# Three transformer blocks on one core: a reordered launch, and the rounding of weights in two halves

## The chip, the core and the metric

One Trainium2 chip, one of its cores. The time is the device time of one execution in microseconds (us), the median of the runs. TensorE (PE) multiplies, VectorE (DVE) and ScalarE (ACT) work element by element, GpSimd (POOL) rounds the weights, and SyncE (SP) only issues transfers. An engine waits for another on a semaphore.

## The reference, cut to what matters

Three residual blocks run over a sequence of 512 tokens with 1024 features, in fp32. The start of the first block is what the launch computes:

```python
def rmsnorm(x, g):
    y = xf * lax.rsqrt(jnp.mean(xf * xf, axis=-1, keepdims=True) + EPS)
    return (y * g).astype(x.dtype)

def short_conv_mixer(xn, w_in, conv_w, w_out):
    b, c, h = jnp.split(xn @ w_in, 3, axis=-1)
    return (b * causal_dwconv(c * h, conv_w)) @ w_out
# block 1: x += short_conv_mixer(rmsnorm(x)); x += conv_ffn(rmsnorm(x))
# block 2: forgetting attention (16 heads, own k/v norm), conv_ffn
# block 3: gated linear attention and sliding-window attention (8 heads, sinks), merged by
#          two sigmoid gates, w_out; then a gated feed-forward layer
```

The matrices hold about 186 MB in all, and each is read once.

## The kernel before, in words

Activations are kept with features on the 128 partitions: XT[:, m, :] is feature tile m (128 features) by 512 tokens, eight tiles in all. An fp32 product is made of three fast products: every operand is split into a high part rounded to fp32r and a low part, the rest. XH and XL are the split of x times the norm's gain; the factor of each token, rsqrt(mean(x*x)), is applied later, to the result of a product, as the row W[0].

A weight unit is [128, 8 x 128] (some have 6 x 128): 354 of them. For each, SP loads it into RAW[slot] (L439) when the slot's last unit is split, POOL makes the high part (L468, one operand), waits for its own semaphore `high_done`, makes the low part (L470, two operands) and then raises `split_done`; POOL waits for `unit_done` before it writes a ring slot again. The ring has four slots, in some phases three. In loops POOL also issues one tiny operation (L467). PE's `unit` (L485 to 487) takes 8 x 3 matmuls of 512 columns.

The launch is written out by hand, in this order of each engine's queue:

- SP: four loads of x (XIN, 512 KB each), then the units' weights.
- ACT: the load of the constants (CST), 18 small loads of parameters (L1523) into the rows PROW and one more (L1524); then `residual("_x")`: for each tile a square (L1149) and a high part XH (L1151); then `norm("_x")`.
- PE: three transposes of PROW after all the parameters have come; then for each tile m four transposes (L1098) of XIN into bank m % 2, each pair of banks freed by DVE's copy; then the first products of the loop `mix`, whose three units per step go to banks 0, 1 and 2. After the first unit, `row_sums` (L498) adds up the squares over the partitions.
- DVE: constants, parameters (L2153 to 2159), then for each tile: the copy of PS into XT (L2165), the sum of squares (L1587, L1590), the low part XL (L1593); then the norm (L1567, Newton's step L1557 and L1558, with ACT's Ln, Exp, Square at L1131 to 1133 between).

PE may begin the first unit when `resid` counts all eight copies.

The prediction also speaks of one place of the sliding-window part: for head group g and block q, `swa_scores`, DVE's maximum (L2007), small sums (L2010, L2016, L2017), four scalings of the probabilities SPROB (L2019), then PE's transposes of these (L974, `swa_turn_probs`). Around it DVE also does norms of q and k (L1966, L1969).

## Time and profile before

| | |
|---|---|
| median of 3 runs | 2167.97 us (2167.3 to 2170.32) |
| the profiled execution | 2167.74 us, of which the span of the trace is 2165.7 us |
| PE busy | 2119.7 us (98%) |
| POOL busy | 1285.0 us (59%), 907 instructions |
| DVE busy | 1164.8 us (54%), 1520 instructions |
| ACT busy | 432.6 us (20%) |
| DMA | 193.44 MB, mean 89 GB/s |

The profile's page gives busy times by engine; busy time of PE is modelled, so idle time and the distance between starts say more than it. Views of the trace: the timeline lists instructions in order of time, the waits who stood idle for whom, the groups by line the mean duration of an operation, the stretches the busy time and the granted TensorE clock in a window.

### The profile page before, as it was taken

To read this page: it belongs to the slowest core of one execution; us is meant where nothing else is said; L and a number is where in the kernel's file an instruction comes from. 1 tells how busy PE (TensorE), PEld (TensorE's weight loads), DVE (VectorE), ACT (ScalarE), POOL (GpSimd) and SP (SyncE) were. 2 spreads that over 40 slices of the span, in tenths; PEclk is the share of its full clock that TensorE was granted. 3 is DMA by queue.
4 is the path that set the end of the run, shared out by engine and by line. 5 is a ranking of instruction groups with operands and counts; after the bars stand their busy time and mean duration, and the time that the engine had idled before them with its cause. 6 is when DMAs were issued, how large, how long until landed. Compare 5 with 4: busy or idle time off the path is not lost.

```text
span 2165.7 us, 29143 instructions
## 1 busy us (share of the span) xinstructions
PE 2119.7 (98%) x10839; PEld 1768.7 (82%) x10847; DVE 1164.8 (54%) x1520; ACT 432.6 (20%) x879; POOL 1285.0 (59%) x907
## 2 busy tenths in 40 slices
PE   5999999999999999999999999999999999999999
PEld 4888888888788887888888888889877888888887
DVE  5557777731546666687762167345754455444200
ACT  2002111100243334211110053222223112111000
POOL 3777766656653344676666755435534666666564
PEclk9999999999999999999999999999999999999999
DMA  4333333323332221333323432223222333333232
GB/s 125 97 107 107 90 96 96 94 81 94 110 109 79 79 79 49 109 100 95 96 73 102 115 85 70 68 59 88 68 64 64 88 100 95 97 97 97 73 97 83
DMA packets 368005, 193.44 MB, mean 89 GB/s; under 512 B 6592, under 2 KB 364320, under 8 KB 367920
## 3 DMA queue, kind: packets, MB, share of 16 engines
q1 hardware_dynamic: 364272, 186.67, 30.0%
q10 hardware_dynamic: 3648, 5.59, 0.8%
q8 instruction: 58, 0.95, 0.2%
q14 instruction: 27, 0.22, 0.0%
HBM read 190.11 MB, written 2.13 MB: 89 GB/s over the span
## 4 chain that ended last, share of the span: by engine, by line
PE 86%; DVE 8%; issue 3%; ACT 2%; ACTq 0%; DMA 0%; DVEq 0%
PE PS L485 20%; PE PS L486 20%; PE PS L487 20%; DVE W L1590 2%; PE PS L762 2%; PE PS L778 2%; PE PS L763 2%; PE PS L764 2%; PE PS L779 2%; PE PS L780 2%; PE PS L664 2%; PE PS L665 2%; PE PS L666 2%; PE PS L578 1%; PE PS L847 1%
## 5 line engine op out<-in xcount | busy, mean ns | idle before, releaser
L470 POOL TENSOR_TENSOR RING<-RAW,RING 128x1024 fp32r<-128x1024 f32 (+1 forms) x354 | 870.2, 2458 | 29.5
L468 POOL TENSOR_SCALAR RING<-RAW 128x1024 fp32r<-128x1024 f32 (+1 forms) x354 | 379.0, 1071 | 518.0 <-PE PS L487 147.8
L485 PE MATMUL PS<-XH,RING 128*128 128x512 f32 x1344 | 526.5, 392 | 5.6 <-DVE XT L2165 2.6
L486 PE MATMUL PS<-XL,RING 128*128 128x512 f32 x1344 | 523.5, 390 | 0.0
L487 PE MATMUL PS<-XH,RING 128*128 128x512 f32 x1344 | 523.5, 389 | 0.0
L485 PEld LDWEIGHTS PS<-XH,RING 128*128 128x128 f32 x1344 | 252.7, 188 | 61.7 <-DVE XT L2165 3.0
L486 PEld LDWEIGHTS PS<-XL,RING 128*128 128x128 f32 x1344 | 252.8, 188 | 53.1 <-issue 1.2
L487 PEld LDWEIGHTS PS<-XH,RING 128*128 128x128 f32 x1344 | 252.7, 188 | 52.7
L467 POOL TENSOR_TENSOR COL<-COL 128x1 f32<-128x1 f32 x195 | 44.9, 230 | 314.7 <-PE PS L487 314.7
L485 PE MATMUL PS<-HH,RING 128*128 128x512 f32 x528 | 205.6, 389 | 0.0
L487 PE MATMUL PS<-HH,RING 128*128 128x512 f32 x528 | 205.4, 389 | 0.0
L486 PE MATMUL PS<-HL,RING 128*128 128x512 f32 x528 | 205.4, 389 | 0.0
L1601 DVE TENSOR_TENSOR XT<-PS,XT 128x512 f32<-128x512 f32 (+1 forms) x48 | 33.2, 692 | 312.8 <-PE PS L487 312.7
L1631 DVE TENSOR_TENSOR HL<-W,HH 128x512 f32 (+1 forms) x66 | 117.2, 1775 | 58.7 <-ACT HH L1166 58.7
L778 PE MATMUL PS<-RING,XH 128*128 128x256 f32 x448 | 129.7, 290 | 0.9 <-DVE SGA L1892 0.9
L779 PE MATMUL PS<-RING,XH 128*128 128x256 f32 x448 | 126.7, 283 | 0.0
L780 PE MATMUL PS<-RING,XL 128*128 128x256 f32 x448 | 126.6, 283 | 0.0
L1163 ACT ACTIVATE W<-W 128x512 f32<-128x512 f32 x66 | 41.8, 633 | 415.2 <-DVE W L1608 341.5
L487 PEld LDWEIGHTS PS<-HH,RING 128*128 128x128 f32 x528 | 99.1, 188 | 20.6
L486 PEld LDWEIGHTS PS<-HL,RING 128*128 128x128 f32 x528 | 99.1, 188 | 20.6
L485 PEld LDWEIGHTS PS<-HH,RING 128*128 128x128 f32 x528 | 99.1, 188 | 20.5
L1607 DVE SCALAR_TENSOR_TENSOR W<-W,FC,W 128x512 f32<-128x512 f32 x44 | 104.0, 2364 | 6.0 <-DVE W L1606 1.7
(299 smaller groups left out, 3385.1 us busy)
## 6 DMA issues: line engine op xcount, KB each, us to landing
RAW<-in_ffn_w_up SPq DMA_DIRECT2D x88, 512.0 KB, 3.7
RAW<-in_w_in SPq DMA_DIRECT2D x53, 512.0 KB, 3.7
RAW<-in_w_ffn_in SPq DMA_DIRECT2D x44, 512.0 KB, 3.8
RAW<-in_ffn_w_down SPq DMA_DIRECT2D x32, 512.0 KB, 4.0
RAW<-in_a_w_in SPq DMA_DIRECT2D x24, 512.0 KB, 3.7
RAW<-in_w_kvf SPq DMA_DIRECT2D x17, 512.0 KB, 4.0
RAW<-in_b_w_qg SPq DMA_DIRECT2D x16, 512.0 KB, 3.7
RAW<-in_w_ffn_out SPq DMA_DIRECT2D x16, 512.0 KB, 3.8
```

The source lines that it names most:

```text
L467: pool.tensor_tensor(TICK, ONEC, ONEC, ALU.mult)
L468: pool.tensor_scalar(WH[s][:, 0:nk, :], RAW[s][:, 0:nk, :], 1.0, 1.0, ALU.mult, ALU.mult).then_inc(high_done, 1)
L470: pool.tensor_tensor(WL[s][:, 0:nk, :], RAW[s][:, 0:nk, :], WH[s][:, 0:nk, :].bitcast(F32), ALU.subtract).then_inc(split_done, 1)
L485: pe.matmul(o, WH[s][:, k, :], xh[:, k0 + k, :], start=first and k == 0, stop=False)
L486: pe.matmul(o, WH[s][:, k, :], xl[:, k0 + k, :], start=False, stop=False)
L487: mm = pe.matmul(o, WL[s][:, k, :], xh[:, k0 + k, :], start=False, stop=last and k == nk - 1)
L664: pe.matmul(o, xh[:, k, c], RING[:, s:s + 2, 0, k, :], start=k == 0, stop=False)
L778: pe.matmul(o, XH[:, k, c], RING[:, s:s + 2, 0, k, :], start=k == 0, stop=False)
L779: pe.matmul(o, XH[:, k, c], RING[:, s:s + 2, 1, k, :], start=False, stop=False)
L780: mm = pe.matmul(o, XL[:, k, c], RING[:, s:s + 2, 0, k, :], start=False, stop=k == KT - 1)
L1607: link(dve.scalar_tensor_tensor(o, x[:, 1:S + 1], w[1], o, ALU.mult, ALU.add))
L1631: dve.tensor_tensor(tile(HL, m), g, tile(HH, m).bitcast(F32), ALU.subtract).then_inc(sem("ffn_low"), 1)
```

## The change

Two edits. The first reorders the launch. SP issues the first weight unit, then the four x loads, then the other units; each x load has a semaphore of its own. The 16 rows of `attn_norm` get a buffer GROW and a load right after the constants. PE transposes them into bank 7, then transposes x block by block of 128 tokens as each arrives, into all eight banks; nothing frees a bank in between. XH and XL are made straight from PSUM: ACT squares the first three token blocks (128 x 1024, summed along the row by the instruction), then makes the eight XH, then squares the fourth block. DVE makes XL from PSUM and later copies PSUM into XT ("keep"), six tiles; ACT copies two. The token factor is computed on [128, 4] values and brought to a row by a product of ones with a diagonal matrix, after the second unit. The other parameters are transposed after the first unit, in bank 3. Tests on semaphores are renumbered (`tables`, `params`, `prm_ready`), with no other effect.

The second edit is in POOL's loop: k tiles 0 to 3 and 4 to the end are rounded one after the other, high, low, high, low, each with its wait; `split_done` comes after the second low part.

The core of the diff (renumbered waits and allocations left out):

```diff
@@ sync
+            def load_x():
+                for t in range(TB):
+                    sp.dma_start(XIN[:, t, :], ...).then_inc(sem(f"x_loaded{t}"), 16)
             for p in ph.values():
 ...
+                        if p is ph["mix"] and isinstance(i, int) and i == j == 0:
+                            load_x()
@@ gpsimd
-                        pool.tensor_scalar(WH[s][:, 0:nk, :], RAW[s][:, 0:nk, :], 1.0, 1.0, ALU.mult, ALU.mult).then_inc(high_done, 1)
-                        pool.wait_ge(high_done, p.unit(i, j) + 1)
-                        pool.tensor_tensor(WL[s][:, 0:nk, :], RAW[s][:, 0:nk, :], WH[s][:, 0:nk, :].bitcast(F32),
-                                           ALU.subtract).then_inc(split_done, 1)
+                        for h, (k0_, k1) in enumerate(((0, 4), (4, nk))):
+                            hi = pool.tensor_scalar(WH[s][:, k0_:k1, :], RAW[s][:, k0_:k1, :], 1.0, 1.0, ALU.mult, ALU.mult)
+                            hi.then_inc(high_done, 1)
+                            pool.wait_ge(high_done, p.unit(i, j) * 2 + (h + 1))
+                            lo = pool.tensor_tensor(WL[s][:, k0_:k1, :], RAW[s][:, k0_:k1, :],
+                                                    WH[s][:, k0_:k1, :].bitcast(F32), ALU.subtract)
+                            if h:
+                                lo.then_inc(split_done, 1)
@@ tensor
-            pe.wait_ge(sem("params"), 16 * N_PARAM_DMAS)
 ...
-            for m in range(KT):
-                if m >= 2:
-                    pe.wait_ge(sem("resid"), tiles("_x") + m - 1)
-                for t in range(TB):
-                    tr = pe.transpose(PS[:, m % 2, t * P:(t + 1) * P], XIN[:, t, m * P:(m + 1) * P], ...)
-                tr.then_inc(sem("xt"), 1)
+            pe.wait_ge(sem("consts"), 32)
+            pe.transpose(PS[:, 7, 0:2 * KT], GROW[:, :], ...).then_inc(sem("prm_t"), 1)
+            for t in range(TB):
+                pe.wait_ge(sem(f"x_loaded{t}"), 16)
+                for m in range(KT):
+                    if t == 0 and m == KT - 1:
+                        pe.wait_ge(sem("prm_ready"), 2)
+                    tr = pe.transpose(PS[:, m, t * P:(t + 1) * P], XIN[:, t, m * P:(m + 1) * P], ...)
+                    if t == TB - 1:
+                        tr.then_inc(sem("xt"), 1)
-            pe.wait_ge(sem("resid"), tiles("_x") + KT)
+            def param_rows():
+                pe.wait_ge(sem("params"), 16 * (N_PARAM_DMAS + 1))
+                pe.wait_ge(sem("zeroed"), 1)
+                pe.wait_ge(sem("kept_v"), 2)
+                for l in range(3):
+                    tr = pe.transpose(PS[:, 3, P * l:P * l + P], PROW[:, l, :], CST[:, C_ID:C_ID + P])
+                tr.then_inc(sem("prm_t"), 1)
             def mix(i):
+                first = isinstance(i, int) and i == 0
                 for j in range(3):
+                    if first:
+                        pe.wait_ge(*((sem("kept_v"), 1), (sem("kept_s"), 1), (sem("kept_s"), 2))[j])
 ...
+                    unit(p, i, j, j, XH, XL, ready=(sem("xld"), 1, 0) if first and j == 0 else None)
+                    if first and j == 0:
+                        param_rows()
+                    if first and j == 1:
+                        pe.wait_ge(sem("diag"), TB)
+                        pe.wait_ge(sem("kept_v"), 6)
+                        pe.matmul(PS[:, 7, :], ONE[:, :], DIAG[:, :], start=True, stop=True).then_inc(sem("nsum"), 1)
@@ scalar
             act.dma_start(CST[:, :], T["consts"][:, 0:C_GF]).then_inc(sem("consts"), 16)
+            act.dma_start(GROW[:, :], T["attn_norm"].rearrange("l (k p) -> (l k) p", p=P)).then_inc(sem("consts"), 16)
 ...
-            residual("_x", 1, KT, [(XH, XL, R_ATTN)])
-            norm("_x")
+            def square_x(t):
+                act.wait_ge(sem(f"x_loaded{t}"), 16)
+                act.activation(SQX[:, t, :], XIN[:, t, :], ACT.Square, accum_out=XSS[:, t:t + 1]).then_inc(sem("x_sq"), 1)
+            for t in range(3):
+                square_x(t)
+            act.wait_ge(sem("prm_ready"), 2)
+            for m in range(KT):
+                act.wait_ge(sem("xt"), m + 1)
+                act.activation(XH[:, m, :], PS[:, m, :], ACT.Copy, scale=PRM[:, R_ATTN + m:R_ATTN + m + 1]).then_inc(sem("xhd"), 1)
+            square_x(3)
+            rsqrt(XSS, XR, XRR, sem("nv"), 1, sem("nrr"))
+            for m in (1, 2):
+                act.wait_ge(sem("xld"), m + 1)
+                act.copy(XT[:, m, :], PS[:, m, :]).then_inc(sem("kept_s"), 1)
@@ vector
-            residual("_x", 1, KT, [(XH, XL, R_ATTN)], take_x, ahead=True)
-            norm("_x")
+            dve.tensor_copy(PRM[:, R_ATTN:R_ATTN + 2 * KT], PS[:, 7, 0:2 * KT]).then_inc(sem("prm_ready"), 1)
+            dve.wait_ge(sem("prm_ready"), 2)
+            def keep(m):
+                dve.tensor_copy(XT[:, m, :], PS[:, m, :]).then_inc(sem("kept_v"), 1)
+            for m in range(KT):
+                dve.wait_ge(sem("xhd"), m + 1)
+                dve.scalar_tensor_tensor(XL[:, m, :], PS[:, m, :], PRM[:, R_ATTN + m:R_ATTN + m + 1],
+                                         XH[:, m, :].bitcast(F32), ALU.mult, ALU.subtract).then_inc(sem("xld"), 1)
+                if m == 0:
+                    keep(0)
+            dve.wait_ge(sem("x_sq"), TB)
+            dve.tensor_scalar(XSS, XSS, 1.0 / D, EPS, ALU.mult, ALU.add).then_inc(sem("nv"), 1)
+            keep(3)
+            keep(4)
+            keep(5)
+            newton(XSS, XR, XRR, sem("nrr"), 1, XR)
+            for t in range(TB):
+                dve.tensor_scalar(DIAG[:, t * P:(t + 1) * P], IDF[:, :], XR[:, t:t + 1], None, ALU.mult).then_inc(sem("diag"), 1)
+            keep(6)
+            keep(7)
+            dve.wait_ge(sem("prm_t"), 2)
 ...
+            dve.wait_ge(sem("nsum"), 1)
+            link(dve.tensor_copy(W[0][:, 0:S], PS[:, 7, :]))
```

## Rows read from the trace of the kernel before

**Rows 1.** The page, busy time by engine.

```profile
PE 2119.7 (98%) x10839; PEld 1768.7 (82%) x10847; DVE 1164.8 (54%) x1520; ACT 432.6 (20%) x879; POOL 1285.0 (59%) x907
```

**Rows 2.** Waits of PE: line, waited for, us in total, times, longest.

```profile
PE PS L1088 <- DMA PROW<-in_ffn_conv: 12.9, 1, 12.9
PE PS L1098 <- DVE XT L2165: 7.0, 5, 3.0
PE PS L974 <- DVE SPROB L2019: 5.7, 1, 5.7
PE PS L664 <- DVE KN L1685: 2.2, 1, 2.2
```

**Rows 3.** Timeline of the launch: start, duration, engine, line, operation, idle before.

```profile
8.44 0.36 ACTq L1524 DMA_DIRECT2D TINY<-in_swa_sinks  x1
11.27 1.05 POOL L468 TENSOR_SCALAR RING<-RAW 128x1024 fp32r<-128x1024 f32 x1 [10.82 <-DMA RAW<-in_a_w_in]
14.91 1.28 ACT L1149 ACT_TABLE_LOAD   x1 [14.91 <-DVE PRM L2159]
16.21 0.63 ACT L1149 ACTIVATE W<-XT 128x512 f32<-128x512 f32 x1
16.74 0.71 ACT L1151 ACTIVATE XH<-XT,PRM 128x512 fp32r<-128x512 f32 x1
24.48 0.74 DVE L1593 SCALAR_TENSOR_TENSOR XL<-XT,PRM,XH 128x512 fp32r<-128x512 f32 x1
31.46 0.80 PE L485 MATMUL PS<-XH,RING 128*128 128x512 f32 x1 [2.61 <-DVE XT L2165]
```

**Rows 4.** The same timeline: POOL's tiny operation, released by a unit's last matmul.

```profile
39.00 0.20 POOL L467 TENSOR_TENSOR COL<-COL 128x1 f32<-128x1 f32 x1 [16.86 <-PE PS L487]
45.24 0.19 POOL L467 TENSOR_TENSOR COL<-COL 128x1 f32<-128x1 f32 x1 [2.56 <-PE PS L487]
50.68 0.19 POOL L467 TENSOR_TENSOR COL<-COL 128x1 f32<-128x1 f32 x1 [1.75 <-PE PS L487]
```

**Rows 5.** ACT's groups by line and shape: busy us, mean ns, idle before.

```profile
L1220 ACT ACTIVATION_READ_ACCUMULATOR PROB<-PROB,COL 128x1 f32 x64 | 12.0, 187 | 0.0
L1131 ACT ACTIVATE TINY<-TINY 128x8 f32<-128x8 f32 (+1 forms) x26 | 5.3, 206 | 58.5 <-DVE TINY L1676 32.8 <-DVE TINY L1969 25.7
```

**Rows 6.** POOL's groups by line and shape, columns as in rows 5.

```profile
L470 POOL TENSOR_TENSOR RING<-RAW,RING 128x1024 fp32r<-128x1024 f32 x330 | 825.4, 2501 | 27.5
L468 POOL TENSOR_SCALAR RING<-RAW 128x1024 fp32r<-128x1024 f32 x330 | 358.8, 1087 | 511.6 <-PE PS L487 141.3 <-PE PS L780 118.2 <-PE PS L666 112.8
L470 POOL TENSOR_TENSOR RING<-RAW,RING 128x768 fp32r<-128x768 f32 x24 | 44.8, 1866 | 2.0
L468 POOL TENSOR_SCALAR RING<-RAW 128x768 fp32r<-128x768 f32 x24 | 20.2, 842 | 6.4 <-PE PS L487 6.4
```

**Rows 7.** Timelines of DVE, POOL and PE in the sliding-window part.

```profile
1558.50 1.60 DVE L1969 SCALAR_TENSOR_TENSOR TINY<-TINY 128x4 f32<-128x4 f32 x1
1565.26 1.85 DVE L2016 TENSOR_TENSOR COL<-COL 128x4 f32<-128x4 f32 x1
1567.35 6.94 DVE L2019 TENSOR_SCALAR SPROB<-SPROB,COL 128x384 f32<-128x384 f32 x4
1643.27 1.41 DVE L2019 TENSOR_SCALAR SPROB<-SPROB,COL 128x384 f32<-128x384 f32 x4
1567.05 1.05 POOL L468 TENSOR_SCALAR RING<-RAW 128x1024 fp32r<-128x1024 f32 x1
1571.73 2.34 POOL L470 TENSOR_TENSOR RING<-RAW,RING 128x1024 fp32r<-128x1024 f32 x1
1574.34 2.82 PE L974 MATMUL PS<-IDF,SPROB 128*128 128x128 f32 x12 [5.68 <-DVE SPROB L2019]
1648.99 1.47 PE L974 MATMUL PS<-IDF,SPROB 128*128 128x128 f32 x12
```

**Rows 8.** Stretch 1573 to 1578: busy us by engine, granted clock, DMA share, GB/s.

```profile
1573.00:1578.00 5.00, 3.66 (x15) 3.46 (x16) 3.17 (x4) 1.17 (x2) 1.07 (x1) 0.52 0.57 149
```

More of the change, by code:

```diff
@@ L218, in build @@
         CST = at("CST", [P, C_GF], F32, BIG + 18 * KB)
+        SQX = at("SQX", [P, TB, D], F32, BIG + 64 * KB)
+        GROW = at("GROW", [2 * KT, P], F32, W_at[9])
+        DIAG = at("DIAG", [P, S], F32, W_at[3])
+        XSS, XR, XRR = [TINY[:, c:c + TB] for c in (48, 52, 56)]
         BUH = at("BUH", [P, KT, S], F32R, BIG + 32 * KB)
@@ L550, in body @@
                             unit(pu, i, 2 * q + k, 2 * q + k, XH, XL,
-                                 ready=(sem("xld"), 1, tiles(n)) if isinstance(i, int) and i == 0 and q == k == 0 else None)
+                                 ready=(sem("xld"), 1, scaled(n)) if isinstance(i, int) and i == 0 and q == k == 0 else None)
                             if isinstance(i, int) and i == 0 and q == k == 0:
@@ L692, in attention @@
                 pe.wait_ge(sem("resid"), tiles(1) + KT)
-                unit(p, 0, 0, 0, XH, XL, ready=(sem("xld"), 1, tiles(1)))
+                unit(p, 0, 0, 0, XH, XL, ready=(sem("xld"), 1, scaled(1)))
                 row_sums(1)
@@ L886, in gla @@
                 pe.wait_ge(sem("resid"), tiles(3) + KT)
-                unit(ph["lr"], 0, 0, 4, XH, XL, ready=(sem("xld"), 1, tiles(3)))
+                unit(ph["lr"], 0, 0, 4, XH, XL, ready=(sem("xld"), 1, scaled(3)))
                 row_sums(3)
@@ L1106, in mix @@
                         pe.wait_ge(sem(f"mix_{'chb'[j]}"), i * 1)
-                    unit(p, i, j, j, XH, XL, ready=(sem("xld"), 1, tiles("_x")) if isinstance(i, int) and i == 0 and j == 0 else None)
-                    if isinstance(i, int) and i == 0 and j == 0:
-                        row_sums("_x")
+                    unit(p, i, j, j, XH, XL, ready=(sem("xld"), 1, 0) if first and j == 0 else None)
[5 more added lines that the diff above has]
+                        pe.matmul(PS[:, 7, :], ONE[:, :], DIAG[:, :], start=True, stop=True).then_inc(sem("nsum"), 1)
@@ L1135, in norm @@
             def norm(n):
-                rsqrt(W[4][:, 0:S], W[5][:, 0:S], W[6][:, 0:S], sem("nv"), ORDER[n] + 1, sem("nrr"))
+                rsqrt(W[4][:, 0:S], W[5][:, 0:S], W[6][:, 0:S], sem("nv"), ORDER[n] + 2, sem("nrr"))
             def residual(n, iters, tpi, gains):
@@ L2207, in PARAM_DMAS @@
     d = []
-    for row, a in ((R_ATTN, T["attn_norm"]), (R_FFN, T["ffn_norm"]), (R_ACONV, T["a_conv"][0])):
+    for row, a in ((R_FFN, T["ffn_norm"]), (R_ACONV, T["a_conv"][0])):
         n = a.shape[0] * a.shape[1] // P
@@ L2224, in PARAM_DMAS @@
     return d
-N_PARAM_DMAS = 3 + 8 + 4 + 1 + 2
+N_PARAM_DMAS = 2 + 8 + 4 + 1 + 2
 def constants():
```

57 lines of the change are left out of this document (25 added, 32 removed).

## The prediction, made before the changed kernel was run

> **What bounds the kernel now.** I read the page first: PE is busy for 98% of the span [rows 1], so 46 us of the 2165.7 are all that can be had without fewer matmuls. The waits of PE come next: the two longest lie in the launch, for the last small parameter load and for DVE's copies out of PSUM, and behind them stand one wait of 5.7 us for SPROB and one of 2.2 for KN [rows 2]. Then the timeline of the launch: the first product starts at 31.46 [rows 3], and POOL's tiny operation, which starts right after a unit's last matmul, marks the ends of the first three units at 39.00, 45.24 and 50.68 [rows 4]. So a unit costs 50.68 - 45.24 = 5.44 us when nothing stops it, and the row sum between the first two costs 6.24 - 5.44 = 0.8. Nowhere in PE's waits does POOL stand as the cause: beside the four of [rows 2] there are 14 groups, of 0.2 to 2.6 us, and they name DVE or only issue. Last, the timeline of the one long wait later on [rows 7].
>
> The time outside the span is 2167.74 - 2165.7 = 2.0 us and stays. The profiled execution lies 0.2 us under the median.
>
> **Part 1, the launch.** What it removes: PE's wait for 18 parameter loads ahead of x, the eight rounds through two banks, the sum of squares on DVE (eight operations, some of them long), and the copy into XT ahead of XL. What takes its place is a chain through ACT, which I add up in time.
>
> - x. W0, x and the constants are the same bytes that before had landed when POOL began at 11.27 [rows 3]; only their order is turned round. So the last x block lands at about 11.2. POOL gets W0 ahead of the first x block and has split it long before 15; nobody waits for that.
> - ACT issues its loads until 8.44 + 0.36 = 8.80 [rows 3]; the load of GROW takes the place of another. Its table load is 1.28: until 10.1. In before it came right after a wait; here it may be ahead of it, which changes nothing since block 0 is there by then.
> - Three squares of 128x1024. No such row exists. A square of 512 takes 0.63 [rows 3], twice that is 1.26 from above; the start of the next one 0.53 later (16.21 to 16.74, rows 3) gives 1.06 from below; with 0.19 for the read of the sum [rows 5], if it isn't overlapped, 1.06 to 1.45. I take 1.3: until 14.0. The last x block is transposed by then: 8 transposes behind 11.2.
> - Eight XH at 0.53 apart to 0.71 each [rows 3], taken as 0.6: until 18.8. The first one is there at 14.7, DVE's first XL (0.74, rows 3) at 15.5, and PE can begin the first unit at 15.5 instead of 31.46.
> - Fourth square 1.3 (20.1), table for Ln 1.28 (21.4), Ln 0.21, table for Exp 1.28, Exp and Square 0.21 each (23.3) [rows 3, 5], then the copy of XT tile 1 out of bank 1, 0.6 to 0.7 by the ACT rows of that size: 24.0. The second unit waits for this copy. Queued behind ACT's squares are XH, and so DVE and PE; behind the rsqrt are the two copies.
>
> PE's own path to that point: the first unit from 15.5. It took 39.00 - 31.46 = 7.5 us before [rows 3, 4], against 5.44 when nothing stops it; DVE's XL (eight of 0.74 and one keep of about 0.7) set no less than 6.6 + 0.7. Until 22.8 to 23.0, and three transposes behind, at most 0.9: 23.9. The two paths meet at 24.0, so unit 2 starts at 24.1. It ends at 29.6, the sum by ones and DIAG 0.8, the third unit 5.44: 35.9, against 50.68. **That is 14.8 us.** What could be late inside: DIAG. DVE has newton's results at 23.6, then four operations in SBUF while POOL splits the fourth unit (from 23.0, about 3.7 us), then two keeps: done at 28 if each loses 0.8, at 30 if each loses 1.25. So 0 to 0.5 us on the path; I take 0. The first products are read by DVE after the third unit has started, as before; nothing that follows in the loop depends on when it began. Bounds of part 1: squares and XH at their ends give +-1.6; DIAG 0.5; PE as the later path 1. So 12 to 16.5 us.
>
> **Part 2, POOL's halves.** Price on POOL: from 1024 to 768 columns the low part falls from 2501 to 1866 ns and the high part from 1087 to 842 [rows 6]: 2.48 and 0.96 ns per column, the fixed part 0 and 0.1. Two halves are thus 2 x (1.24 + 0.60) = 3.7 against 3.59, and one more wait for its own semaphore, 0.1 at most. POOL's unit becomes 3.7 to 4.0 us, 354 of them 40 to 140 us more work. Who covers it: PE needs 5.44 per unit [rows 4]; POOL is idle for 880 us of the span [rows 1]. So nothing on the path, while the cover holds. If it didn't, each unit would cost the difference.
>
> Gain on DVE: at 1567.35 the four scalings of SPROB last 6.94 us; the same four last 1.41 at 1643.27 [rows 7]. In between POOL rounds two units without a pause, from 1567.05 to 1571.73 + 2.34 = 1574.07, and DVE's last one ends at 1574.29. Four POOL operations, four DVE operations: each of DVE's gets in only where one of POOL's ends. With pieces of half the length the four get in within 3.6 to 3.9 us, 3.2 less. Ahead of them in the same chain stand operations on four elements that last 1.60 and 1.85 [rows 7]; they too lose about half, 1.6 together. DVE is ready 4.8 us earlier, and PE's wait of 5.68 shrinks to about 0.9. The wait had a second price: in the window behind it the granted clock was 0.52 [rows 8], the same 12 transposes lasted 2.82 instead of 1.47 [rows 7], and some matmuls behind them ran slower too: 1.3 to 1.8 us, which a wait of 0.9 wouldn't bring. Against it: the first weight unit of that part is split only when the doubles before it are done, so POOL's longer unit can hold PE by 0 to 0.5 once; but then PE comes later to the wait for SPROB, so it is in the sum already. **About 6 us**, between 2 and 7.5. The other waits for DVE, KN [rows 2] and twelve smaller ones, some 11 us together, are behind chains of which only a part is held by POOL: 0.8 us, between -1 and 3.
>
> What the trace shows of the price of DVE's getting in: POOL's two units took 7.02 us in that stretch, no more than 2 x 3.59 by their means. DVE's four operations cost it nothing.
>
> The Trainium skill's page "SBUF — State Buffer" (section "SBUF: two separate sides") says that DVE and GpSimd share a port pair that is locked for a whole instruction, by whichever starts first, and that the other is fully blocked. For DVE the rows agree. By the same rule POOL would be blocked at each of its doubled boundaries as well, which speaks against the change: with it the sum would be that of the third rival, below. The 7.02 us do not show it.
>
> **Sum.** 2167.74 - 14.8 - 6 - 0.8 = 2146.1; against the median, 2146.4.
>
> **Rivals.**
>
> *The halves bring nothing.* DVE's chain is then as long as before, because POOL's pieces are back to back and DVE is held by the next one as well, or what DVE wins POOL loses. For it: the chain has ACT operations between DVE's. Against it: four for four in the rows. Time: 2167.97 - 14.8 = 2153, from 2151 to 2156.
>
> *The launch brings much less.* The ACT chain is the new bound, and it is all in one queue. If the parameters' wait comes back (GROW behind the constants and x), or ACT's squares wait for late blocks because W0 is ahead of x, everything moves by that; Against it: W0 is 0.5 of the 2.9 MB that have landed by 11.27, so each block comes at most 2 us later than before, and the third still ahead of its square at 12.7. A further table load in the chain would be 1.28. Launch 9 to 12, halves as forecast: 2149 to 2153.
>
> *Slower: POOL becomes the bound in the feed-forward phases.* There DVE has, per two units, five operations that work in SBUF alone, each of the size of XL's 0.74 [rows 3] or less. If each of them blocks POOL at a boundary, POOL's two units take 2 x 3.85 + 5 x 0.7 = 11.2 us, and PE's 10.88. It decides from 5.44 us per unit on. The loss is 0.16 us and, with loop overhead, perhaps 0.3 for each of about 200 feed-forward units: 32 to 60 us, less the launch: 2167.97 - 14.8 + 32 = 2185 and up. Against it: the 7.02 us, and that POOL idles 512 us ahead of its high parts alone, and more ahead of its tiny operation, released by PE [rows 4, 6].
>
> This is what the Trainium skill's rule on the port pair, named above, would give if it held for POOL as it does for DVE.
>
> *More.* Several of the ten small waits go and the chain on ACT is at its lower ends: 2138 to 2141.
>
> **How the numbers follow.** Forecast 0.60 (2141 to 2150), halves without effect 0.17, launch with less 0.12, more 0.07, slower 0.04. The range that leaves out about 2 in 10 and takes in the bounds is 2139 to 2156. A difference of 0.2%, 4.3 us, is about what a measurement of this kernel tells from none. Faster by more: 0.94; within: 0.02; slower: 0.04.
>
> **What would show it.** In the profile after: the first product near 15.5 and POOL's tiny operations ending the first units near 23, 29.7 and 36; ACT's squares at 1.1 to 1.4 us; the second unit released by ACT's copy or just behind the three transposes. POOL's pieces near 0.6 and 1.24 us, with more busy time but no waits of PE for POOL; the four scalings of SPROB below 4.2 us, and PE's wait there near 1. Wrong would be: a first unit after 18; a second unit held past 25; PE waits on POOL; SPROB's wait over 3.

## The result, and the profile after

The changed kernel takes 2137.76 us (median of 4 runs, 2137.62 to 2138.7) against 2167.98 for the kernel before in the same session; the ratio is 0.9858, with a 95% interval of 0.9845 to 0.9872. The profiled span fell from 2165.7 to 2135.9 us, by 29.8. The forecast was 2146.4 with a range from 2139 to 2156, so the result lies 1.2 us below the range: the sign and the two main mechanisms were right, one term was much too small.

The page after, busy time by engine, to be read against [rows 1]:

```profile
PE 2113.4 (99%) x10840; PEld 1766.9 (83%) x10848; DVE 968.7 (45%) x1516; ACT 431.5 (20%) x881; POOL 1503.7 (70%) x1615
```

DVE does nearly the same instructions and is busy for 196 us less; POOL is busy for 219 us more. Some of the longest waits of PE after (line, waited for, us in total, times, longest), against [rows 2]. KN and QN are the normed keys and queries of the attention, OF its output, YGL the low part of the gated linear attention's output, XN the normed tile of the sliding-window part.

```profile
PE PS L1102 <- DMA GROW<-in_attn_norm: 5.6, 1, 5.6
PE PS L594 <- issue: 2.6, 8, 1.4
PE PS L501 <- DVE XT L2197: 2.0, 1, 2.0
PE PS L658 <- DVE OF L1737: 1.3, 2, 0.7
```

SPROB and KN are gone from the list, POOL is not in it. The launch after, from its timeline (start, duration, engine, line, operation, idle before), against [rows 3, 4]:

```profile
8.22 1.28 ACT L1555 ACT_TABLE_LOAD   x1 [8.22 <-issue]
10.57 1.04 ACT L1555 ACTIVATE SQX<-XIN 128x1024 f32<-128x1024 f32 x1
11.62 1.04 ACT L1555 ACTIVATE SQX<-XIN 128x1024 f32<-128x1024 f32 x1
12.65 4.71 ACT L1561 ACTIVATE XH<-PS,PRM 128x512 fp32r<-128x512 f32 x8
14.85 0.80 PE L501 MATMUL PS<-XH,RING 128*128 128x512 f32 x1 [2.02 <-DVE XT L2197]
21.58 1.05 ACT L1566 COPY XT<-PS 128x512 f32<-128x512 f32 x2
22.26 0.48 PE L501 MATMUL PS<-XH,RING 128*128 128x512 f32 x1
28.07 0.19 POOL L479 TENSOR_TENSOR COL<-COL 128x1 f32<-128x1 f32 x1 [1.48 <-PE PS L503]
34.40 0.47 POOL L479 TENSOR_TENSOR COL<-COL 128x1 f32<-128x1 f32 x1 [2.22 <-PE PS L503]
```

The first product starts at 14.85 instead of 31.46, and POOL's tiny operation marks the end of the second unit at 28.07 and of the third at 34.40, instead of 45.24 and 50.68.

Where the 29.8 us lie can be read by setting matmul k of one trace beside matmul k of the other, since both kernels issue the same products from there on. The start of a matmul in before, less that in after:

```
behind the launch (217 us of before)          16.6
KN wait, 612.8                                +2.4
QN and the smaller waits up to 846            +0.9
XL wait, 890.3                                +1.1
YGL wait, 1334.1                              +1.3
XN, 1525.7                                    +0.2
first unit of the merge, 1560.2               -0.7
SPROB wait, 1574.3                            +5.9
low clock behind it, to 1577.8                +1.7
the rest                                      +0.4
                                              ----
                                              29.8
```

The line "QN and the smaller waits" is a net: 1.0 at QN and 0.5 at 845 us, less 0.3 at each of three waits for OF, which grew from 1.1 to 2.1 us together. So the launch gave 16.6, the sliding-window place 6.9, and all other waits together 6.3, where the forecast had 14.8, 6 and 0.8.

### The profile page after: what moved, and what is told of

Same layout as the page of the kernel before. It is cut to its first block, busy times and chain, and to the rows that moved or that the text cites. A ratio compares the mean times of both kernels' runs of the same rounds, so it can differ in the third digit from the quotient of the medians.

```text
span 2135.9 us, 30007 instructions
## 1 busy us (share of the span) xinstructions
PE 2113.4 (99%) x10840; PEld 1766.9 (83%) x10848; DVE 968.7 (45%) x1516; ACT 431.5 (20%) x881; POOL 1503.7 (70%) x1615
## 4 chain that ended last, share of the span: by engine, by line
PE 96%; DVE 2%; ACT 1%; issue 0%; DMA 0%; DVEq 0%; SPq 0%; ACTq 0%
PE PS L501 23%; PE PS L502 23%; PE PS L503 23%; PE PS L778 2%; PE PS L794 2%; PE PS L780 2%; PE PS L779 2%; PE PS L795 2%; PE PS L796 2%; PE PS L680 2%; PE PS L682 2%; PE PS L681 2%; PE PS L594 1%; PE PS L625 1%; PE PS L982 1%; PE PS L1001 1%
## 5 line engine op out<-in xcount | busy, mean ns | idle before, releaser
L484 POOL TENSOR_TENSOR RING<-RAW,RING 128x512 fp32r<-128x512 f32 x708 | 967.7, 1367 | 59.1
L481 POOL TENSOR_SCALAR RING<-RAW 128x512 fp32r<-128x512 f32 x708 | 513.9, 726 | 408.2 <-PE PS L796 105.3
L503 PEld LDWEIGHTS PS<-HH,RING 128*128 128x128 f32 x528 | 99.1, 188 | 20.6
L1666 DVE TENSOR_TENSOR W<-PS,W 128x512 f32<-128x512 f32 x66 | 45.6, 690 | 146.9 <-PE PS L503 146.8
L1660 DVE TENSOR_TENSOR W<-PS,W 128x512 f32<-128x512 f32 x66 | 45.6, 691 | 127.4 <-PE PS L503 127.3
```

What stands on the lines that cost most here:

```text
L481: hi = pool.tensor_scalar(WH[s][:, k0_:k1, :], RAW[s][:, k0_:k1, :], 1.0, 1.0, ALU.mult, ALU.mult)
L484: lo = pool.tensor_tensor(WL[s][:, k0_:k1, :], RAW[s][:, k0_:k1, :], WH[s][:, k0_:k1, :].bitcast(F32), ALU.subtract)
L503: mm = pe.matmul(o, WL[s][:, k, :], xh[:, k0 + k, :], start=False, stop=last and k == nk - 1)
L1660: dve.tensor_tensor(a[:, 2:S + 2] if with_conv else u, PS[:, 2 * q, :], W[0][:, 0:S], ALU.mult).then_inc(sem("ffn_a"), 1)
L1666: dve.tensor_tensor(g, PS[:, 2 * q + 1, :], W[0][:, 0:S], ALU.mult).then_inc(sem("ffn_g"), 1)
```

## Experiments

All twelve kernels were timed in runs beside the kernel before, each session with its own median of it (2168 to 2170 us); the ratio is given. Where an experiment concerns POOL's pieces, its edit is this one, with other cut points or for some of the phases alone:

```diff
-                        for h, (k0_, k1) in enumerate(((0, 4), (4, nk))):
+                        for h, (k0_, k1) in enumerate(p.pieces(nk)):   # cut points per phase; semaphore counts follow
```

### Each part alone

The new launch with POOL's units whole (no cut), and the launch of before with the halves (cut at 4).

> The new launch with POOL's rounding whole, as before. The changed kernel is 16.6 us ahead of the one before in the first feed-forward layer and 29.8 us at its end; the question is where the 13.2 us behind the launch are from. Theory 1 (DVE's chains are held by POOL's long instructions, place by place): all 13.2 us go, the lead of 16.6 stays constant to the end, 2151.3 us, and PE's waits for SPROB (5.7 us) and KN (2.2) are there again. Theory 2 (the launch moved DVE, POOL and PE against each other and some of the waits fell out by that): the lead grows behind the launch, 2147 us or less, and one of the two waits is shorter.

> The kernel before with POOL's halves alone. Theory 1: 13.2 us, 2154.8, and no lead before the attention part; the parts add up with the launch alone within 1 us. Theory 2: less than 10 us, 2158 or more.

The launch alone takes 2152.95 us (2151.72 to 2153.48), ratio 0.9923 (0.9907 to 0.994), span 2151.4. The halves alone take 2154.6 us (2153.76 to 2155.03), ratio 0.9933 (0.9917 to 0.995), span 2152.0. By ratio the parts add up, 0.77% and 0.67% against 1.42% for both. The spans of the profiled executions fall by 14.3 and 13.7, together 28.0 of the 29.8. With the launch alone the two long waits are back:

```profile
PE PS L1002 <- DVE SPROB L2071: 5.6, 1, 5.6
PE PS L692 <- DVE KN L1737: 2.2, 1, 2.2
```

With the halves alone they are gone, though everything happens 16 us later in time. So it is not a shift of phase between engines that removed them; it is the halves. The wait of 0.7 for QN is an exception: it is gone with the launch alone as well (0.8 gained there, 1.0 with the halves alone), so each of the two edits takes it away. Of the 1.8 that the sum of the spans lacks, 0.8 lies in the launch itself: the first product behind the short convolution starts at 164.68 before, 149.19 with the launch alone, and 148.40 after. The launch alone is worth 15.5, and the halves inside it 0.8: a 128x4 operation of DVE, which lasts 1.18 us beside one of POOL's whole subtractions and 0.16 in the kernel after, puts off Ln and with it the second unit. The rest lies in the execution with the launch alone: it loses 1.5 behind the wait for KN and 0.7 behind the one for SPROB, both times to a low clock, and gains 1.0 at QN and later.

### Where the halves must be: at each held operation of the chain, however far from the wait

PE's wait for KN stands at 612.8 us of before. DVE's last operations ahead of it are short, [rows 2] names only KN itself, and I had judged the wait by them. But the chain begins earlier. DVE in the kernel before, up to 23 us ahead of the wait's end:

```profile
589.52 2.34 DVE L1557 SCALAR_TENSOR_TENSOR W<-W,W 128x512 f32<-128x512 f32 x1 [3.31 <-ACT W L1133]
594.61 2.44 DVE L1734 TENSOR_SCALAR W<-W,PRM 128x512 f32<-128x512 f32 x1
601.73 1.52 DVE L1742 SCALAR_TENSOR_TENSOR W<-W,W 128x512 f32<-128x512 f32 x1 [3.54 <-ACT W L1268]
603.28 1.95 DVE L1744 TENSOR_TENSOR_SCAN W<-W,W 128x512 f32<-128x512 f32 x1
```

and the last three of the same in the kernel after:

```profile
576.79 0.76 DVE L1774 TENSOR_SCALAR W<-W,PRM 128x512 f32<-128x512 f32 x1
582.23 0.69 DVE L1782 SCALAR_TENSOR_TENSOR W<-W,W 128x512 f32<-128x512 f32 x1 [3.52 <-ACT W L1294]
582.96 1.52 DVE L1784 TENSOR_TENSOR_SCAN W<-W,W 128x512 f32<-128x512 f32 x1
```

They lost 1.7, 0.8 and 0.4 us. Two kernels test it. The four units that POOL rounds over this stretch (the first four of the phase "quads", 587 to 607 us of before) are the only ones left whole in the kernel after; and they are the only ones in halves in the launch alone.

```diff
+                return [(0, 4), (4, nk)] if not (name == "quads" and j < 4) else [(0, nk)]   # four whole
+                return [(0, 4), (4, nk)] if (name == "quads" and j < 4) else [(0, nk)]       # four in halves
```

> The kernel after, but the four units of the attention that POOL rounds between 587 and 607 us of the kernel before (the first four of the quads, 10 to 25 us ahead of PE's wait for KN) are rounded whole again; every unit near the wait itself (from 610 us of before on) stays in halves. Upstream theory (POOL's long instructions hold the links of DVE's chain well before the wait: L1557 2.34 us, L1734 2.44, L1742 1.52, L1744 1.95): PE's wait for KN is back at 2 to 2.4 us, the profiled span 2 to 3 us above that of the kernel after, ratio to before 0.9858 + 0.0011, about 0.987. Last-link theory (what I predicted by: only the two or three DVE operations just ahead of the wait matter): no wait for KN, the time of the kernel after within 0.5 us.

> The new launch with POOL whole, and only those four units of the quads in halves. Upstream theory: PE's wait for KN (2.2 us in the new launch alone) is gone or below 0.5 us, the span 2 to 3 us below that of the new launch alone, about 2150.5 us (ratio 0.991), with DVE's busy time almost that of the new launch alone (1155 us less at most 5). Last-link theory: KN's wait stays at 2.2, ratio 0.992. The waits for SPROB (5.6) and YGL (1.1) stay by both.

Four whole: 2142.95 us (2142.22 to 2143.57), ratio 0.9879 (0.9864 to 0.9894), span 2141.8, 5.9 above the kernel after. Four in halves: 2149.41 us (2148.22 to 2150.47), ratio 0.9909 (0.9896 to 0.9923), span 2147.6, 3.8 below the launch alone; DVE's busy time is 1153.6 against 1155.3. PE's waits with the four whole:

```profile
PE PS L691 <- DVE KN L1736: 2.9, 1, 2.9
```

Here the three operations last 2.43, 1.50 and 1.95 us again. In the other kernel the wait for KN is gone. Four of 354 units make or remove it, and none of those near the wait itself. For KN the last-link reading is refuted. The size of the first experiment was more than I expected, and its trace says why. These are stretches of it, with busy time by engine (and instructions), then the granted clock, the DMA share and GB/s:

```profile
592.00:596.00 4.00, 2.09 (x18) 1.89 (x16) 2.03 (x4) 1.71 (x5) 1.73 (x2) 1.00 0.86 262
596.00:603.00 7.00, 5.96 (x29) 5.99 (x29) 4.46 (x7) 0.63 (x3) 5.72 (x7) 0.51 0.29 77
```

Behind the wait of 2.9 us the granted clock was 0.51, and until 602.8 the matmuls went on 0.21 us apart, where those of the kernel after went on 0.12 apart: 3.1 us for the wait and 2.6 for the clock. In the kernel before, the wait of 2.2 us at the same place brought no such stretch: its matmuls went on 0.12 us apart. The kernel with the four in halves fell by 3.8: set beside the launch alone, operation by operation, it is 0.4 ahead until 580 us and 4.2 from 600 us on, and 0.4 of that is lost again later, so the place is worth 3.8. The wait is 2.2 of it and the clock again the rest: the launch alone had a granted clock of 0.72 from 596 to 602 us, where the kernel with the four in halves had 1.00.

The waits for XL, YGL and QN show that the distance differs from chain to chain. At XL's it is nothing: the last two operations ahead of the wait at 890.3 us are themselves the held ones, before and after:

```profile
886.11 2.71 DVE L1590 TENSOR_TENSOR W<-W,W 128x512 f32<-128x512 f32 x1 [0.75 <-ACT W L1149]
888.74 1.53 DVE L1593 SCALAR_TENSOR_TENSOR XL<-XT,PRM,XH 128x512 fp32r<-128x512 f32 x1
```

```profile
866.22 1.17 DVE L1630 TENSOR_TENSOR W<-W,W 128x512 f32<-128x512 f32 x1 [0.75 <-ACT W L1175]
867.31 1.09 DVE L1633 SCALAR_TENSOR_TENSOR XL<-XT,PRM,XH 128x512 fp32r<-128x512 f32 x1
```

For YGL they are a multiplication and a scan, 2 to 7 us ahead, which fell from 1.35 to 0.92 and from 3.29 to 2.19; for QN two scalings of probabilities, 5 to 9 us ahead, from 1.10 to 0.42 and from 2.32 to 0.52. No run tests those two places by themselves.

### Length or number of pieces

Three cuts, all with the new launch everywhere: unequal pieces of 1 and 7 k tiles (cut at 1); the high part whole and only the subtraction in two; four pieces (cuts at 2, 4 and 6). In the expectation of the first, L is the theory that the length of the piece that DVE meets counts, N that the number of boundaries does.

```diff
-                        for h, (k0_, k1) in enumerate(((0, 4), (4, nk))):
-                            hi = pool.tensor_scalar(WH[s][:, k0_:k1, :], RAW[s][:, k0_:k1, :], 1.0, 1.0, ALU.mult, ALU.mult)
+                        pool.tensor_scalar(WH[s][:, 0:nk, :], RAW[s][:, 0:nk, :], 1.0, 1.0, ALU.mult, ALU.mult).then_inc(high_done, 1)
+                        pool.wait_ge(high_done, p.unit(i, j) + 1)
+                        for k0_, k1 in ((0, 4), (4, nk)):              # subtraction only in two
```

> The changed kernel with POOL's pieces of 1 and 7 k tiles in place of 4 and 4: as many instructions and boundaries, but the longest is about 2.1 us instead of 1.3. Theory L (DVE loses by the length of POOL's instruction): for an operation that comes at a random time, the mean wait is the sum of squared lengths over twice their sum: 1.04 us whole, 0.53 in halves, 0.75 here; so DVE's busy time is half way between 1165 and 969 us, near 1055, and the time 2142 to 2146. Theory N (it is the number of boundaries at which DVE gets in): as the changed kernel, DVE near 970 us, 2138 to 2139.

> The kernel after, but with the high part of each unit made in one piece (1.07 us) and only the subtraction in two: three instructions for POOL. By the theory that the length of the instruction that DVE meets sets its loss: the subtractions (2.4 us whole, 1.3 in halves) are the long ones, so nearly all of the gain of the halves stays: DVE's busy time about 1000 us (968.7 with both in halves, 1155 with none), the waits for SPROB, KN and QN gone, time within 0.15% of the kernel after (ratio 0.985 to 0.987). By the theory that the number of places at which DVE can come in counts (three of them between pieces against four), a third of the halves' 14 us is lost: ratio about 0.988. POOL's busy time falls to about 1420 us.

> The changed kernel with POOL's rounding in four pieces. Theory L: mean wait of DVE 0.27, its busy time down another 90 to 100 us to about 870; POOL's unit is 4.6 to 4.9 us, still below PE's 5.44, so PE never waits for POOL, and as only about 2 us of PE's waits are left that hang on held DVE operations, 2136 to 2138. Rival (cover gone: unit splits come late where units are freed in pairs, or POOL is over 5.44 in the feed-forward layers where DVE gets in most): PE waits for POOL, 2145 or more.

```
                       us        ratio (95%)               DVE busy  POOL busy  SPROB's four scalings
whole (launch alone)   2152.95   0.9923 (0.9907-0.994)     1155.3    1283.3     6.94
subtraction in two     2145.26   0.9892 (0.9877-0.9907)    1032.0    1401.6     5.17
1 and 7                2145.02   0.9892 (0.9876-0.9909)    1134.2    1451.8     4.10
halves (after)         2137.76   0.9858 (0.9845-0.9872)     968.7    1503.7     3.88
quarters               2175.91   1.003  (1.0018-1.0043)     886.2    1764.6     2.55
```

The last column is the place of [rows 7], in us as the others are. Neither theory is enough by itself. The time with 1 and 7 is what L forecast (2142 to 2146; its runs spread from 2142.68 to 2147.36, and the waits below are of the fastest). DVE's total goes with the length of POOL's pieces and not with their number: with 1 and 7 it is nearly as busy as with whole units, though there are as many boundaries as with halves. But the formula of L gave 1055 for it, 79 too few. SPROB's four scalings follow the number of boundaries: 4.10 with four uneven pieces and 3.88 with four even ones, but 5.17 with three and 6.94 with two. That fits the picture of [rows 7]: a lone operation of DVE waits for the rest of the piece it meets; of several in a row each gets in at one boundary. No run tests this picture apart from these totals. What each cut leaves: With 1 and 7 the waits for KN and SPROB are gone and those for OF (2.4, 1.3) and XN (2.5) grow; with the subtraction in two KN still costs 2.0 and SPROB 1.6, and 0.9 is lost at a place of the gated linear attention. My expectation for that one, within 0.15% of the kernel after, was wrong by 0.2 points, since it counted length alone.

The quarters (2175.09 to 2176.99, span 2174.6) are the slower rival of the prediction come true. POOL in the feed-forward layer with quarters, its tiny operation that stands ahead of each unit:

```profile
251.12 0.19 POOL L490 TENSOR_TENSOR COL<-COL 128x1 f32<-128x1 f32 x1
256.92 0.19 POOL L490 TENSOR_TENSOR COL<-COL 128x1 f32<-128x1 f32 x1
262.85 0.19 POOL L490 TENSOR_TENSOR COL<-COL 128x1 f32<-128x1 f32 x1
```

It never waits for PE there, a unit takes 5.80 to 5.93 us, and PE, which needs 5.44, follows: 0.42 us lost for each unit. PE's list shows it as many short waits:

```profile
PE PS L513 <- POOL RING L496: 7.4, 40, 0.2
PE PS L692 <- POOL RING L496: 2.3, 1, 2.3
```

The same stretch of the kernel after, where POOL still waits for PE, but only just:

```profile
300.59 1.61 POOL L484 TENSOR_TENSOR RING<-RAW,RING 128x512 fp32r<-128x512 f32 x1
302.59 0.20 POOL L479 TENSOR_TENSOR COL<-COL 128x1 f32<-128x1 f32 x1 [0.39 <-PE PS L503]
302.74 0.62 POOL L481 TENSOR_SCALAR RING<-RAW 128x512 fp32r<-128x512 f32 x1
305.02 1.06 POOL L481 TENSOR_SCALAR RING<-RAW 128x512 fp32r<-128x512 f32 x1
306.16 1.30 POOL L484 TENSOR_TENSOR RING<-RAW,RING 128x512 fp32r<-128x512 f32 x1
308.03 0.19 POOL L479 TENSOR_TENSOR COL<-COL 128x1 f32<-128x1 f32 x1 [0.58 <-PE PS L503]
```

In this stretch halves leave POOL 0.4 to 0.6 us in each unit of 5.44. That is the whole cover of this change.

### Where in the kernel the halves, or quarters, are worth it

> The new launch, with halves only in the units from the attention's gates to the first merge (107 of the 366 units or so), and POOL whole in the launch, the short convolution, the three feed-forward layers, the output product behind the second merge and the second merge itself. By the theory that the gain of the halves is made only where a chain of DVE ends in a wait of PE (KN, QN, OF, XL, YGL, SPROB), and that the 107 us of DVE's time saved elsewhere lies behind PE anyway: the time of the kernel after plus the 0.7 us by which the launch with whole pieces was behind, plus at most 0.5 for XL and the last product: ratio 0.986 to 0.987, DVE busy about 1080 us, all of those waits gone. By the theory that the halves in the feed-forward layers are worth something of their own: 3 us or more above the kernel after, ratio 0.9875 or more.

Halves only from the attention's gates to the first merge, 95 of 354 units (not 107 of 366, as the expectation has it): 2140.65 us (2140.4 to 2142.21), ratio 0.9871 (0.9855 to 0.9888), span 2140.4, DVE 1135.6 where I had expected 1080. Set beside the kernel after, matmul by matmul, it is 2.5 us behind at the end of the launch, 1.2 more at the XL wait ahead of the second feed-forward layer, and 0.3 and 0.4 at the same place ahead of the first and the third. POOL rounds that layer's units ahead of time, here whole, and the two operations shown above last 2.71 and 1.53 us again. The 2.5 is more than the 0.7 I had put there; most of it is the clock, as the last section shows. So the ratio came out just over my bound, while the halves outside the middle part, with 167 us of the 187 of DVE time that all of them save, brought 1.9 us ahead of the three layers, up to 0.8 in the launch, and nothing inside the layers.

> The kernel after, but units of the attention, of the gated linear attention, of the sliding window and of the first merge in four pieces; the short convolution, the feed-forward layers, the output products and the second merge stay in halves. By the theory that four pieces lose only where POOL's cover ends (5.44 us a unit in the feed-forward layers, where POOL had 0.4 to 0.6 us to spare in halves, and quarters cost PE 0.35 us a unit): the feed-forward layers keep the halves' time, the waits left for DVE in the other stages (XN 0.7, OF 2.1) get shorter; but in the gated linear attention, where PE also works through units at full length, POOL is the bound and some of the loss of quarters stays. Estimate: +3 us (0 to +12) against the kernel after, ratio 0.987. By the theory that shorter is better wherever the feed-forward layers are left alone: -1 to -3 us, ratio 0.985. The stage is told by the waits for POOL: if there are none before 560 us and some from 580 us on, the bound moves with the rate of units, not with the name of the stage.

Quarters in that middle part and halves elsewhere: 2138.87 us (2138.19 to 2140.7), ratio 0.9865 (0.9849 to 0.9882), span 2137.2. The launch is 1.35 behind the kernel after, though its pieces there are the same. Behind the launch it loses 1.3 at 585 us, where PE waits 1.2 for POOL, and 0.7 at the first unit of the merge; it gains 0.3 to 0.4 at each of three later places of the attention and 1.2 at three waits for XN. The sum behind the launch is about nothing. By place both my expectations missed: there is no loss in the gated linear attention, and no gain on balance. The time, 1.1 us above the kernel after, does lie in the first one's bounds.

### The launch: the order on ACT and the order of the loads

> The kernel after with all four squares of x behind ACT's eight XH. By my theory of the launch (ACT is one chain: 1.05 us a square, 0.59 an XH): the first XH is held by the transposes instead of ACT, about 12.7 us minus up to 1, since ACT is free from 9.5 but the last x tile's transposes end near 12.6: first product 14.8 or earlier by at most 0.7 us; the fourth square ends at 21.3 instead of 18.3, Ln and Exp near 24.5, ACT's two copies that release the second unit at 25.2 to 25.7 instead of 23.3, so the second unit starts 2.3 to 3 us later and nothing gives that back: about +2.5 us, ratio 0.9870. Rival: the second unit is held by the three parameter transposes at 22 us or by its own split anyway, and ACT's chain has slack: no more than +0.5 us, ratio 0.986.

```diff
-            for t in range(3):
-                square_x(t)
...
-            square_x(3)
+            for t in range(0, TB):
+                square_x(t)
```

All four squares behind the XH: 2144.5 us (2143.38 to 2144.81), ratio 0.9886 (0.9871 to 0.9901), span 2142.8, 6.9 above the kernel after. ACT and PE in its launch:

```profile
13.44 1.28 ACT L1559 ACT_TABLE_LOAD   x1 [13.44 <-PE PS L1108]
14.74 4.74 ACT L1559 ACTIVATE XH<-PS,PRM 128x512 fp32r<-128x512 f32 x8
16.95 0.65 PE L501 MATMUL PS<-XH,RING 128*128 128x512 f32 x1 [2.58 <-DVE XT L2196]
26.80 1.06 ACT L1565 COPY XT<-PS 128x512 f32<-128x512 f32 x2
27.42 0.80 PE L501 MATMUL PS<-XH,RING 128*128 128x512 f32 x1 [2.34 <-ACT XT L1565]
```

I had expected 2.5 us and a first product no later than before. What I left out is the table load: it stands behind the wait of the first operation that needs it. With squares first it ran at 8.22, in the shadow of the transposes; with XH first it stands behind x's last transposes, and 1.28 us come on the path at 13.44. The first product is 2.1 late and the second unit 5.2. The second unit ends 6.7 late (34.81 instead of 28.07): the other 1.6 is the clock, which fell inside this unit, 0.57 granted from 27 to 31 us, where nothing covers it.

> The kernel after with two squares of x ahead of ACT's eight XH instead of three (the other two behind them), and ACT's two copies that release the second and third unit moved ahead of Ln, Exp and their two table loads. By the theory of ACT as one chain in which the table load stays in the shadow of the wait for x: squares end at 11.6, XH runs 11.6 to 16.3, the first product starts at 13.9 instead of 14.85, the fourth square ends at 18.4, the copies at 18.5 to 19.6, so the second unit is held by the first unit's own products and the parameter transposes, about 21.2 instead of 22.26, and the diagonal is ready 1.05 us later (24.4 against the third unit's end near 33), which costs nothing. About -1.0 us, ratio 0.9854. Rival: the second unit follows DVE's chain (XL, then the kept tiles) and not ACT's: the second unit moves by less than 0.3 us, ratio 0.9858. A loss would show that the first product's transposes are late (the fourth tile of x).

```diff
-            for t in range(3):
+            for t in range(2):
...
-            square_x(3)
-            rsqrt(XSS, XR, XRR, sem("nv"), 1, sem("nrr"))
+            square_x(2)
+            square_x(3)
             for m in (1, 2):
                 act.wait_ge(sem("xld"), m + 1)
                 act.copy(XT[:, m, :], PS[:, m, :]).then_inc(sem("kept_s"), 1)
+            rsqrt(XSS, XR, XRR, sem("nv"), 1, sem("nrr"))
```

2136.95 us (2136.76 to 2137.52), ratio 0.9854 (0.9838 to 0.9871), span 2135.7: 0.2 us below the kernel after, no difference that can be told, where I had expected 1.0. Three rows of it:

```profile
12.86 4.74 ACT L1561 ACTIVATE XH<-PS,PRM 128x512 fp32r<-128x512 f32 x8 [1.25 <-PE PS L1108]
15.06 0.50 PE L501 MATMUL PS<-XH,RING 128*128 128x512 f32 x1 [1.29 <-DVE XT L2198]
27.57 1.10 PE L1135 MATMUL PS<-DIAG,ONE 128*128 128x512 f32 x2 [0.72 <-DVE XT L2198]
```

ACT, free at 11.6, waits 1.25 for x's transposes, so the third square had cost nothing. The second unit does start 1.1 earlier (its parameter transposes at 20.87), and most of that is lost again at the row sum, which waits for DVE's kept tiles behind the diagonal. ACT, PE and DVE are level in this launch.

> The kernel after with the four loads of x ahead of the first weight tile on SP's queue, as in the kernel before. By my step in the prediction (x ahead delays the first weight tile, so its split; weights ahead delay x by little): x's transposes start up to 1.5 us earlier (6 instead of 6.95 at best, since GROW lands at 5.6 in any case), but ACT's chain (free at 8.2, squares to 12.6, XH to 17.3) does not start earlier; the first weight tile lands at 9.5 to 11 instead of 5.9, its split ends at 13.4 to 15 instead of 9.86, so the first product is at 14.85 to 15.3. Together 0 to +0.7 us, ratio 0.986. If instead the first product is held by the split at 17 or later, the order of the loads was worth 2 us or more, ratio 0.9868 or above.

```diff
+            load_x()
             for p in ph.values():
 ...
-                        if p is ph["mix"] and isinstance(i, int) and i == j == 0:
-                            load_x()
```

x's loads ahead of the first weight tile: 2138.96 us (2138.83 to 2139.08), ratio 0.9864 (0.9848 to 0.9881), span 2137.1, 1.2 above the kernel after. The weight tile's split starts at 11.22 instead of 5.93 and still does not hold the first product (15.46). The 0.6 us of that come from ACT, whose table load starts at 8.85 instead of 8.22 since its own loads were issued later. The rest comes at the second unit: Ln waits 0.74 us for DVE's 128x4 operation, which lasts 1.10 beside POOL here and 0.16 in the kernel after. The order of the loads is worth about 1 us, not by the way I had named.

## Why the prediction was right, and where it was wrong

**The launch, forecast 14.8, measured 16.6 (15.5 by itself).** The chain through ACT was the right one. Its terms: ACT was free at 8.22, not 8.80; a square of 1024 columns costs 1.05, the lower of my two ends, since the read of the sum overlaps, where I took 1.3; XH is 0.59 each, as taken. First product 14.85 against 15.5, second unit 22.26 against 24.1, end of the third 34.4 against 35.9. The halves' own part in it, 0.8, had no term in my sum; I had looked for held DVE operations only at DIAG (0 to 0.5, taken as 0), and the one that counts stands ahead of Ln.

**SPROB, forecast 6, measured 6.9.** The four scalings lasted 3.88 (forecast below 4.2), the wait went (forecast about 0.9), the low clock behind it gave 1.7 (1.3 to 1.8), and the first unit of the merge cost 0.7 where I had up to 0.5. The same matmuls as in [rows 7], after:

```profile
1546.67 1.47 PE L990 MATMUL PS<-IDF,SPROB 128*128 128x128 f32 x12
```

**The other waits, forecast 0.8 with bounds -1 and 3, measured 6.3. This is the step that failed.** Its terms are 2.4 for KN, 0.9 for QN and small ones, 1.1 for XL, 1.3 for YGL, 0.6 for the rest. I wrote that these chains are held by POOL only in part, and put a small size on all of them without pricing their operations one by one. The runs show that the held part is what PE waited for. For KN it lies 8 to 23 us ahead of the wait, and four units decide it, none of them near it. For XL it is the last two operations, and with whole units there they lose their time again. For YGL and QN the trace shows held operations that got shorter, 2 to 9 us ahead, without a run of their own; and the new launch takes QN's away as well. With 6.3 in place of 0.8, and the launch and SPROB as measured, my own sum gives 2167.74 - 16.6 - 6.9 - 6.3 = 2137.9, against 2137.76. With the 0.8 it would give 2143.4, so the two other terms, 1.8 and 0.9 too small, do not by themselves leave the range.

**POOL's price, forecast 40 to 140 us more work, measured 219.** I claimed that DVE's getting in cost POOL nothing, from 7.02 us for two units against a mean of 3.59. At that place it is true: POOL's four pieces last 1.05, 2.35, 1.15 and 2.34 us beside the four scalings, 0.1 more than undisturbed. But I took it for the rule, and elsewhere the rows show two levels for each piece: in the one above, 0.62 or 1.06 for the high part of 512 columns and 1.30 or 1.61 for the low part. Counted over the trace, about 400 pieces of the kernel after stand at the higher level against about 130 before, 100 us more. The rest, some 120, is the fixed part of a piece: undisturbed, two halves take 3.82 us (0.62 and 1.29, twice) and a whole unit 3.44 (1.05 and 2.39). I had read 3.7 and 3.59 out of means that held both levels. It changed nothing in the sum, since 0.4 to 0.6 us of cover were left, but I had counted on 1.6. The rival to which I gave 4% was nearer than that: quarters met it. The Trainium skill's page "SBUF — State Buffer", section "Who interferes with whom", says that whichever of the two starts first has the shared ports for the whole instruction and the other is fully blocked. DVE's rows agree with it, and so do POOL's pieces at the higher level; the 0.1 us beside the scalings does not show it. I was wrong to set it aside for POOL on the strength of that one place.

## What to carry to other kernels

When one engine's long instructions hold another's, judge a wait by its whole chain and price every link that the long instructions can reach, the last as well as those 20 us ahead; a short last link says nothing. Cut the long instructions until the runs of held operations get through, and no further than the engine's cover per unit allows: here two pieces gained some 15 us over whole units (2152.95 to 2137.76) and four lost some 23 (to 2175.91). In a launch, put a cheap operation of the right table ahead of the first long wait.

## What the runs showed of the hardware

**Which DVE instructions are held.** Those that read PSUM never are: in the kernels before, after, with 1 and 7 and with quarters none of them lasts over 0.15 us more than the fastest of its line and shape. Groups of DVE (busy us, mean ns, idle before) in the kernel before, after and with quarters:

```profile
L1631 DVE TENSOR_TENSOR HL<-W,HH 128x512 f32 x60 | 108.3, 1805 | 54.5 <-ACT HH L1166 54.5
L1626 DVE TENSOR_TENSOR W<-PS,W 128x512 f32<-128x512 f32 x66 | 45.5, 690 | 107.1 <-PE PS L487 105.3
```

```profile
L1671 DVE TENSOR_TENSOR HL<-W,HH 128x512 f32 x60 | 50.1, 835 | 54.5 <-ACT HH L1192 54.5
L1666 DVE TENSOR_TENSOR W<-PS,W 128x512 f32<-128x512 f32 x66 | 45.6, 690 | 146.9 <-PE PS L503 146.8
```

```profile
L1683 DVE TENSOR_TENSOR HL<-W,HH 128x512 f32 x60 | 44.0, 734 | 54.5 <-ACT HH L1204 54.5
L1672 DVE TENSOR_TENSOR W<-PS,W 128x512 f32<-128x512 f32 x66 | 45.7, 692 | 139.2 <-PE PS L515 139.1
```

With one input in PSUM the mean is 690 to 692 ns in all of them; with both in SBUF it falls from 1805 to 835 and 734. This would have told me ahead which links of each chain the halves can shorten.

**What a meeting costs POOL.** The high part of 256, 512 and 1024 columns lasts 0.40, 0.62 and 1.05 us undisturbed and mostly 0.84, 1.06 and 1.50 where DVE is met: 0.44 us whatever the length. Shorter pieces don't make such a meeting cheaper for POOL. From halves to quarters the meetings hardly grow in number, from about 400 to 430 pieces. What makes quarters cost 261 us more is the fixed part: undisturbed, four pieces of 0.40 and 0.73 take 4.52 us and two of 0.62 and 1.29 take 3.82, which is 230 us over the 330 units of eight k tiles.

**A low clock can be free or cost its whole length.** Two launches, the kernel after and the one with halves only in the middle, by stretches of 4 us:

```profile
14.00:18.00 4.00, 3.15 (x8) 2.51 (x9) 4.00 (x7) 4.00 (x7) 3.83 (x5) 0.60 0.32 96
22.00:26.00 4.00, 4.00 (x20) 3.33 (x19) 3.22 (x12) 0.63 (x2) 3.48 (x5) 1.00 0.47 135
```

```profile
14.00:18.00 4.00, 3.14 (x14) 2.54 (x15) 4.00 (x7) 4.00 (x7) 3.92 (x3) 1.00 0.45 135
22.00:26.00 4.00, 2.83 (x8) 2.26 (x9) 3.69 (x8) 1.57 (x5) 2.37 (x1) 0.72 0.48 138
```

In the first the clock was low (matmuls 0.43 us apart instead of 0.23) until 18.0, inside the first unit. It ran until 22.02, when ACT's copy for the second was about done, so it cost next to nothing. In the second the first unit ran at full clock and was done at 20.6, waited for DVE and ACT until 23.18, and then the clock fell in the second unit, where nothing covers it: that unit ended at 30.59 instead of 28.07. The kernel with four units in halves has the very same launch code and ended that unit at 28.50. The launch alone, with the same launch code too, ended it at 28.86. So one launch program differs by 2 us between executions, which is also why single microseconds between these kernels are read here from places in the trace and not from medians.
